# Fifteen overflow blocks of a mixture-of-experts layer, moved from between the static expert blocks to one branch behind them

## The reference

```python
D_MODEL = 1024; SEQ = 2048; N_GROUPS = 4; EXPERTS_PER_GROUP = 8; N_EXPERTS = 32; TOP_K = 2; EXPERT_FF = 256
def hierarchical_moe(h, w_group, b_group, w_router, b_router, w_up, w_down):
    g_prob = softmax(t @ w_group + b_group)                # top-1 of 4 groups
    p_g, g_idx = lax.top_k(g_prob, 1)
    ...                                                    # top-2 of the 8 experts of that group
    combine = jnp.sum(one_hot(ids, N_EXPERTS) * gate[..., None], axis=1)
    for e in range(N_EXPERTS):
        a, u = jnp.split(t @ w_up[e], 2, axis=-1)
        y = y + combine[:, e:e + 1] * ((silu(a) * u) @ w_down[e])
# x = x + g2 * hierarchical_moe(modulate(rmsnorm(x, norm2_g), sh2, sc2), ...); return rmsnorm(x, final_g)
```

## Time and profile before

| what | us |
|---|---|
| median of the 2 runs shown (1013.27 and 1048.96) | 1031.12 |
| profiled execution, its own time | 1017.43 |
| its span, core 7, the slowest | 1015.7 |
| span of core 6, the shortest | 981.9 |
| TensorE busy on core 7 | 879.5 (87%) |

### The profile page before, as it was taken

The page is one execution under the profiler, slowest core; times in us unless marked ns, Lnnn a source line. Parts: engine busy times, 40 slices in busy tenths (PEclk is TensorE's granted clock), DMA queues, the critical chain, the costliest instruction groups (busy, mean ns, idle before and its releaser), DMA issues. The chain is left out here.

```text
span 1015.7 us, 16550 instructions; the slowest of 8 cores (981.9 to 1015.7 us)
## 1 busy us (share of the span) xinstructions
PE 879.5 (87%) x6340; PEld 501.3 (49%) x6340; DVE 562.8 (55%) x1060; ACT 425.3 (42%) x847; POOL 331.4 (33%) x341
## 2 busy tenths in 40 slices
PE   5788999998999999999996278859898998889694
PEld 2344553444544444444544156546666666667342
DVE  1548747879246346677757843333443344435287
ACT  2335325544555644334324013323343343644395
POOL 2112302444224320000010236654566566565200
PEclk9988999989999999999996579989999899999798
DMA  8995897240106016012029878999999989898485
GB/s 154 206 222 136 144 172 133 43 83 2 42 5 203 2 29 158 22 41 95 32 83 169 161 140 150 188 198 194 207 181 176 194 159 212 146 194 162 145 333 206
DMA packets 41811, 140.19 MB, mean 138 GB/s; under 512 B 14704, under 2 KB 19440, under 8 KB 34563
## 3 DMA queue, kind: packets, MB, share of 16 engines
q0 software_dynamic: 24256, 95.29, 51.8%
q1 hardware_dynamic: 17476, 43.84, 12.8%
HBM read 253.66 MB, written 37.22 MB: 286 GB/s over the span
## 5 line engine op out<-in xcount | busy, mean ns | idle before, releaser
L492 PE MATMUL ps<-sb 128*128 128x512 bf16 (+9 forms) x5248 | 824.3, 312 | 94.0 <-DVE sb L525 22.7
L492 PEld LDWEIGHTS ps<-sb 128*128 128x128 bf16 (+4 forms) x5248 | 433.6, 102 | 450.4 <-issue 109.6
L505 ACT ACTIVATE sb<-ps 128x512 bf16<-128x512 f32 (+3 forms) x599 | 320.2, 583 | 444.7 <-PE ps L492 332.9
L510 DVE TENSOR_TENSOR sb<-ps,sb 128x256 bf16<-128x256 f32 (+4 forms) x222 | 96.9, 443 | 162.1 <-PE ps L492 84.1
L1215 POOL DMA_INDIRECT sb<-hd,sb x94 | 100.8, 1072 | 93.6 <-PE ps L492 39.9
L525 DVE COPY sb<-ps 128x1024 bf16<-128x1024 bf16 (+4 forms) x109 | 73.3, 676 | 99.9 <-PE ps L1227 44.6
L807 POOL TENSOR_TENSOR sb<-sb 128x512 bf16<-128x512 bf16 x60 | 74.3, 1242 | 141.7 <-ACT sb L505 134.6
L1265 POOL DMA_INDIRECT yd<-sb x94 | 99.1, 1054 | 47.9 <-ACT sb L505 23.6
L522 DVE SCALAR_TENSOR_TENSOR sb<-sb 128x1024 f32<-128x1024 f32 (+5 forms) x92 | 97.7, 1072 | 1.6
L507 ACT ACTIVATE sb<-sb 128x1024 bf16<-128x1024 f32 x50 | 52.6, 1052 | 76.5 <-DVE sb L510 45.1
L522 DVE SCALAR_TENSOR_TENSOR sb<-sb,ps 128x512 f32<-128x512 f32 x68 | 46.5, 685 | 59.2 <-PE ps L492 50.8
(11 more groups left out here) (44 smaller groups left out, 165.3 us busy)
## 6 DMA issues: line engine op xcount, KB each, us to landing
sb<-wex POOLq DMA_DIRECT2D x47, 1536.0 KB
sb<-x SPq DMA_DIRECT2D x32, 512.0 KB, 9.7
sb<-wad POOLq DMA_DIRECT2D x12, 1024.0 KB, 16.4
sb<-wsl POOLq DMA_DIRECT2D x8, 1024.0 KB, 20.7
sb<-yd SPq DMA_DIRECT2D x16, 512.0 KB, 5.9
out<-sb SPq DMA_DIRECT2D x16, 512.0 KB, 3.2
sb<-wo SPq DMA_DIRECT2D x8, 512.0 KB, 4.4
hd<-sb SPq DMA_DIRECT2D x16, 256.0 KB, 3.0
```

What stands on the lines that cost most here:

```text
L492: ins = e.matmul(o, lhsT=l, rhs=r, start=s0, stop=s1)
L505: S.op("act", lambda e: e.activation(out=out, in_=in_, func=func, scale=scale), reads=[in_] + list(extra), writes=w)
L510: S.op(eng, lambda e: e.tensor_tensor(out=out, in0=a, in1=b, op=op), reads=[a, b], writes=[out])
```

## The change

`KDYN = 0` takes all overflow blocks out of the weave: `items` is now static 0 to 31, then overflow 0 to 14. Everything that belongs to the overflow blocks is recorded as a region of its own. The scheduler orders three pieces one after the other: what comes before the region, the region, and the rest. In the program of each compute engine the region stands under one branch: the engine loads the flag `eidi[15]` (1 if overflow block 0 is in use) and jumps over the region if it is 0. The region's operations signal on semaphores of their own. At its end GpSimd waits for all of these, and behind it a GpSimd no-op (`join`) stands for the region in the dependencies of what follows. SyncE has nothing in the region.

```diff
+KDYN = 0
...
-        while se < NE or sd < NDYN:
-            if sd < NDYN and (sd + 1) * (NE - 8) <= (se - 8 + 1) * NDYN + NDYN:
+        while se < NE or sd < KDYN:
+            if sd < KDYN and (sd + 1) * (NE - 8) <= (se - 8 + 1) * KDYN + KDYN:
                 items.append(("d", sd)); sd += 1
             else:
                 items.append(("s", se)); se += 1
+        NA = len(items)
+        items += [("d", k) for k in range(KDYN, NDYN)]
...
+                    emit_ops(parts[0])
+                    if parts[1]:
+                        v_ = eng.value_load(self.flag, min_val=0, max_val=1)
+                        with eng.If(v_ > 0):
+                            emit_ops(parts[1])
+                            if e == "pool":
+                                for k, v in rfinal:
+                                    eng.wait_ge(sems[k], v)
+                    emit_ops(parts[2])
...
+        def run_items(lo, hi):
+            for i in range(lo, hi + 1):
+                if i < hi:
+                    U(i)
+                if i + 1 < hi:
+                    T(i + 1)
...
+        run_items(0, NA)
+        for e_ in ("pe", "act", "dve", "pool"):
+            S.op(e_, lambda e: e.nop(), reads=[eidi], writes=[("br", e_)], cost=0.05)
+        r0 = len(S.ops)
+        for i in range(NRING):
+            W(NA + i)
+            if i < 4:
+                G(NA + i)
+        T(NA)
+        run_items(NA, NI)
+        r1 = len(S.ops)
+        join = S.op("pool", lambda e: e.nop(), writes=[("join", 0)], cost=0.05)
+        S.region = (r0, r1, join)
+        S.flag = eidi[0:1, NDYN + KDYN:NDYN + KDYN + 1]
```

More of the change, by code:

```diff
@@ L44, in __init__ @@
         self.cache = {}
+        self.region = None
     def _dsem(self, key):
@@ L144, in order, with _run @@
         n = len(ops)
[L145 to L148, removed]
-            for d in o["deps"]:
-                succ[d].append(i)
+        lo, hi, join = self.region
+        for i in range(hi, n):
+            d = ops[i]["deps"]
+            if i != join and any(lo <= k < hi for k in d):
+                ops[i]["deps"] = set(k for k in d if not lo <= k < hi) | {join}
+        ops[join]["deps"] = set(k for k in ops[join]["deps"] if not lo <= k < hi)
+        st = self._run(list(range(lo)), window, lat, None)
+        order = list(st["out"])
+        order += self._run(list(range(lo, hi)), window, lat, None)["out"]
+        st["out"] = []
+        order += self._run(list(range(hi, n)), window, lat, st)["out"]
+        pos = {i: k for k, i in enumerate(order)}
+        self.model = max(o["end"] for i, o in enumerate(ops) if not lo <= i < hi)
+        self.ops = [ops[i] for i in order]
+        for o in self.ops:
+            o["deps"] = set(pos[d] for d in o["deps"])
+        self.region = (lo, hi, pos[join])
+    def _run(self, ids, window, lat, st):
+        ops = self.ops
+        n = len(ids)
+        succ = {i: [] for i in ids}
+        left = {}
+        at = {}
+        inside = set(ids)
+        for i in ids:
+            o = ops[i]
+            left[i] = 0
+            at[i] = 0.0
+            for d in o["deps"]:
+                if d in inside:
+                    left[i] += 1
+                    succ[d].append(i)
+                elif st is not None:
+                    at[i] = max(at[i], ops[d]["end"] + lat)
         ready = {e: [] for e in self.ENGS}
-        free = {e: 0.0 for e in self.ENGS}
-        at = [0.0] * n
         ev = []
-        rings = {"pool": [[], 0.8], "sp": [[], 0.2]}
-        tprev = 0.0
+        if st is None:
+            st = dict(free={e: 0.0 for e in self.ENGS}, rings={"pool": [[], 0.8], "sp": [[], 0.2]}, t=0.0, out=[])
+        free, rings, out = st["free"], st["rings"], st["out"]
+        tprev = st["t"]
         oldest = 0
+        where = {i: k for k, i in enumerate(ids)}
         done = [False] * n
-        out = []
         def finish(i, end):
@@ L206, in next_dma @@
             return best
-        for i in range(n):
+        for i in ids:
             if left[i] == 0:
-                heapq.heappush(ev, (0.0, 0, i))
+                heapq.heappush(ev, (at[i], 0, i))
         while len(out) < n or any(rings[r][0] for r in rings):
@@ L224, in order @@
                     continue
-                if ready[e][0] > oldest + window:
+                if where[ready[e][0]] > oldest + window:
                     continue
@@ L232, in order @@
                 out.append(i)
-                done[i] = True
+                done[where[i]] = True
                 while oldest < n and done[oldest]:
@@ L241, in order @@
         assert len(out) == n
[L242 to L246, removed]
+        st["t"] = tprev
+        return st
     def emit(self):
@@ L258, in emit @@
                 o["sig"] = True
-        cnt = {e: 0 for e in self.ENGS}
-        dcnt = {}
-        for o in ops:
+        lo, hi, join = self.region
+        cnt = {}
+        for i, o in enumerate(ops):
+            r = "r" if lo <= i < hi else "m"
             if not o["sig"]:
@@ L264, in emit @@
                 continue
[L265 to L271, removed]
-        known = {e: {} for e in self.ENGS}
-        prog = {e: [] for e in self.ENGS}
-        nwaits = 0
-        for o in ops:
+            k = (r, "d", o["dma"]) if o["dma"] is not None else (r, "e", o["eng"])
+            cnt[k] = cnt.get(k, 0) + (16 if o["dma"] is not None else 1)
+            o["tick"] = (k, cnt[k])
+        known = {e: {} for e in self.ENGS}
+        saved = None
+        prog = {e: ([], [], []) for e in self.ENGS}
+        for i, o in enumerate(ops):
+            if i == lo:
+                saved = {e: dict(known[e]) for e in self.ENGS}
+            if i == hi:
+                known = saved
             e = o["eng"]
@@ L284, in emit @@
                 k, v = do["tick"]
+                assert k[0] == "m" or lo <= i < hi
                 if need.get(k, 0) < v:
@@ L292, in emit @@
                 waits.append((k, v))
[L293 to L305, removed]
+            prog[e][0 if i < lo else 1 if i < hi else 2].append((waits, o))
+        final = [(k, v) for k, v in cnt.items() if k[0] == "m" and k != ("m", "e", "sp")]
+        rfinal = [(k, v) for k, v in cnt.items() if k[0] == "r"]
+        assert not prog["sp"][1]
+        self.stats = dict(n_ops=len(ops), cnt=cnt)
+        sems = {k: self.esem[k[2]] if k[:2] == ("m", "e") else self._dsem(k) for k in cnt}
         nc = self.nc
@@ L1275, in build_program @@
         T(0)
[L1276 to L1295, removed]
+        def run_items(lo, hi):
[4 more added lines that the diff above has]
+                    T(i + 1)
+                if i < hi:
+                    F(i)
+                for f_ in over_at.get(i, []):
+                    f_()
+                if i > lo:
+                    Dn(i - 1)
+                    O(i - 1)
+                if i == lo:
+                    G(lo + 4)
+                if i == 12:
+                    sdma(FGt, fg_d.partition_broadcast(128), 'c_fg')
+                if i + 5 < hi:
+                    G(i + 5)
+                if i > lo and i - 1 + NRING < hi:
+                    W(i - 1 + NRING)
+        run_items(0, NA)
[12 more added lines that the diff above has]
+        S.flag = eidi[0:1, NDYN + KDYN:NDYN + KDYN + 1]
         NYT = 8
```

23 lines of the change are left out of this document (11 added, 12 removed).

## The result

The changed kernel takes 1111.5 us (1110.78 and 1112.29), 1.097 times the kernel before with an interval of 1.090 to 1.104. In two later comparisons on other occasions the same kernel came out at 1.084 (1.073 to 1.095) and 1.099 (1.092 to 1.107). It is slower by 85 to 100 us, and the profile says where.

What follows compares the result with a forecast made beforehand. Transfers bound the expert stage's first half and TensorE its end. Static end 918 us, start-up 18.6 and fifteen blocks 93 gave 1029.6 us; with tail 65.4 and 1.7 more, 1097 us; 1075 to 1125 us, or 1070 to 1130 with rivals.

Steps and rivals of the forecast that it cites:

- The cover: Expert stage: 32 static transfers of 10 us each hide nearly all of the 15 overflow blocks' 6.2 us of matmuls.
- 10 us a block: Expert stage: DMA time per static block, read from core 6, against 6.2 us of TensorE.
- The static stage's end: Last static matmuls on core 7: set by transfers, at 918 us, with bounds of 905 and 925 us.
- The tail: From the last expert matmul to the span's end: a constant of some 66 us, taken as 65.4 us in the sum.
- the region's price: Overflow region behind the static stage: 18.6 us of start-up and 93 us for fifteen blocks at 6.2 us.
- the start-up: Region's start: 14.5 us until the first weights land, 18.6 us with second weights and lower clock; bounds 10 and 30 us.
- the second weights: Region on cores with two blocks in use: weights land 8.3 us behind the first, TensorE needs 6.2 us; another 2.1 us.
- the clock: TensorE behind the region's first wait: a few microseconds at half speed, costing about 2 us.
- (c): Rival: interleaving itself held up the transfers; static stage would run at TensorE's pace to 790 us, 969 us in all; chance 0.03.
- (b): Rival: the static stage ends earlier than forecast, at 895 us, making the time 1074 us; chance 0.07.
- (a): Rival: GpSimd's order makes region blocks 7.5 us each, slower than TensorE's pace; 1123 us in all; chance 0.10.
- (d): Rival: the flag reads 0, so the seven cores do not take the branch; 985 us; chance 0.02.

Runs made afterwards that it cites:

- the runs with half the weights: About half of each static block's weights left out from block 6 on, in both kernels: interleaved 998.1 us (0.978), with the region 1007.1 us (0.983).
- gathers-first run: Changed kernel with the gathers of the region's blocks 0 and 1 issued before block 0's weights: 1.098, against 1.099 for the changed kernel beside it.

## Why the prediction was right in kind and short in size

Right: the change makes the kernel slower, by the mechanism that I named. The cover is confirmed by the runs with half the weights and by core 6, whose stage ends no earlier without the overflow blocks. (The 10 us a block divide core 6's 319 us by all 32 weights, though six had been issued by 579 us; the 26 issued from 606.13 to 885.57 us are 11.2 us apart. The sum did not rest on it, since the stage's end was taken from core 6 directly.) The static stage's end: I put 918 us for core 7, which had 906.1 us; the seven have 898 to 920 us. That core 0, the slowest, had 919.8 us is luck. The tail: 65.4 us put, 66.4 us found. The branch is taken on seven cores and skipped on core 6, whose span hardly moved. The join adds nothing to see: 8.4 to 10.0 us from the last expert matmul to the tail on the seven, 8.0 to 10.1 us before on the eight.

Short: the measured time is 14 us above the 1097 us, and the ratio of 1.097 is above the 1.078 that my sum gives over its own execution. The step that failed is the region's price, "18.6 + 93", 111.6 us. On the slowest core it was 124.4 us. Of it,

- the start-up until the first 256-column matmuls was 21.1 us (919.82 to 940.96 us), against my 14.5 us. I let the transposes run beside the weight transfer. They could not: their gather was issued behind the weights and was waited for until 937.86 us, 12.6 us after the weights' issue (I had 10.3 us for those), and the transposes, their copies and 1.22 us of waiting came on top. The gathers-first run shows that the queue's order is only a part of this, and that the two needs add up to the same.
- the fifteen blocks then took 103.3 us on core 0, against 93 + 4.1 for the second weights and the clock. Of these two terms the clock cost 3.0 us, with 0.8 us of it in the transposes (2 us put); core 0 has no second block in use, and on the four cores that have one TensorE has no wait for its weights, so no run shows the 2.1 us. On core 7 the blocks took 96.5 us, close to what I had put. The rest is the slow pace of single cores, some 7 us a block instead of 6.2. I took the price of a block from core 6, the fastest, and the metric goes by the slowest. Core 7 and core 5 had such waits in the trace before too, among those that made them the slowest (8.0 and 5.8 us under "issue", 33.8 and 24.1 us for VectorE's copies and ScalarE). That they are the same thing is argued, not shown, and what makes a core slow stays open. I also expected all seven cores within some 10 us; they lie between 1081.7 and 1110.6 us.

A second, smaller point is the base. My sum stood on an execution of 1017.43 us, and my "6% more" on a median that takes in the 1048.96 us; against the faster run of 1013.27 us the same 1097 us are 8.3%, and 9.7% were measured. And the bounds were added up wrongly: 1097 + 7 + 11 + 6 is 1121 us, not 1125.

Of the rivals, (c), that interleaving itself held up the transfers, is refuted: the static stage alone ran at 186 to 191 GB/s on core 0 from 620 to 900 us, with TensorE idle a quarter of the time, and no core ended it before 898 us, where (c) needed 839 us. (b) came true in part (898 to 906 us on three cores) without being felt, since it did not happen on the slowest. (a) is in part what the slowest core looks like, some 7 us a block (7.5 us put), but it is not GpSimd's pace by its program, since cores 5 and 7 run the same program at 6.2 to 6.4 us. (d) did not happen: seven cores executed the region.

## What to carry to other kernels

Here dead work on one engine that lay between transfers which bound the stage cost little (nothing to see on core 6, 8 to 17 us on the slowest core); moved behind them it cost its full time, 80 to 91 us. Before putting rarely used work under a branch, ask how often the branch is taken on the slowest core: here one block in use of fifteen makes the core execute all of them. Keep the blocks that are likely to be needed woven in, put only the rest behind the branch, and take a block's price from the slowest core.

## What the runs showed that I had not expected

A gather issued behind a 1.5 MB weight transfer on the same queue was used 10 us after its issue, and issuing transfers earlier gave back only 7 to 10 us, where 13 to 20 us were expected. ScalarE stood for 3.0 to 4.5 us behind a jump over fifteen blocks and 0.7 us behind one over thirteen. And the same program region took between 113 and 127 us on different cores of one chip, with time under "issue" on those that took longest, in kernels with and without a branch; in one execution with the gathers first it took up to 146 us.
